# Attention's context: normed by token rows during the last pair of experts, its keys and values multiplied between the norm's transposes

## The reference

```python
x = layer_norm(DEEPNORM_ALPHA * x + g2 * y, ln_ffn_g[layer], ln_ffn_b[layer])   # end of the first block
...
h  = rmsnorm(x, norm_g[i]) * (1 + scale) + shift
hc = rmsnorm(ctx, norm_g[i]) * (1 + cscale) + cshift
a_val, a_gate, q, k, v, b_gate = jnp.split(h @ w_in, EVEN_SPLITS_2, axis=-1)
ck, cv = jnp.split(hc @ w_in[:, EVEN_SPLITS_2[2]:EVEN_SPLITS_2[4]], 2, axis=-1)
```

## Time and profile before

| what | value |
|---|---|
| median of 3 runs (lowest, highest) | 2036.94 us (2034.76, 2041.7) |
| the profiled execution: its own time | 2035.64 us |
| the profiled execution: span | 2033.8 us |
| TensorE busy | 1957.2 us, 96% |
| VectorE busy | 923.7 us, 45% |
| ScalarE busy | 347.5 us, 17% |
| chain that ended last: TensorE, VectorE, issue | 92%, 5%, 1% |

### The profile page before, as it was taken

One profiled execution on the slowest core, in us unless ns is written; L12 is line 12 of the kernel. 1 busy time (PEld: TensorE's weight loads), 2 busy tenths in 40 slices (PEclk: granted clock), 3 DMA queues, 4 the chain that ended last, 5 costly groups with the idle time before them and its releaser, 6 DMA issues.

```text
span 2033.8 us, 23216 instructions
## 1 busy us (share of the span) xinstructions
PE 1957.2 (96%) x8998; PEld 1177.3 (58%) x8998; DVE 923.7 (45%) x1909; ACT 347.5 (17%) x874; POOL 53.9 (3%) x89
## 2 busy tenths in 40 slices
PE   5999999999999989999999999999999989999998
PEld 3886744433433338789967444334333378768875
DVE  6556743422222215768777534222222256653364
ACT  1111311011111103331013110111111131321121
POOL 0100000000000000000000000000000000020000
PEclk9999899999999998999998999999999999999999
DMA  9863588899999974753354888999999866223411
GB/s 405 328 258 133 188 329 361 346 391 423 424 424 420 423 320 151 266 200 132 125 191 187 331 358 346 393 423 423 423 422 423 347 257 235 96 83 132 146 39 42
DMA packets 82107, 576.90 MB, mean 284 GB/s; under 512 B 9148, under 2 KB 11452, under 8 KB 12800
## 3 DMA queue, kind: packets, MB, share of 16 engines
q1 hardware_dynamic: 70992, 494.84, 60.1%
q0 software_dynamic: 10992, 80.43, 10.8%
HBM read 574.17 MB, written 1.06 MB: 283 GB/s over the span
## 4 chain that ended last, share of the span: by engine, by line
PE 92%; DVE 5%; issue 1%; DMA 1%; ACT 1%; DVEq 0%; SPq 0%
PE ps L301 90%; PE ps L305 2%; DVE hma L514 1%; DVE slab L313 1%; DVE slab L1258 0%; DMA slab<-in_ada 0%; DVE hma L313 0%; DVE gds L655 0%; DVE slab L2800 0%; DVE slab L2797 0%; DVE slab L2590 0%; ACT slab L308 0%; DMA wbuf<-in_od_out 0%; DVE wbuf L480 0%; DVE wP L2054 0%
## 5 line engine op out<-in xcount | busy, mean ns | idle before, releaser
L301 PE MATMUL ps<-slab 128*128 128x256 f32 (+7 forms) x1960 | 580.0, 465 | 3.3 <-DVE slab L2074 2.1
L301 PE MATMUL ps<-wbuf,slab 128*64 128x512 f32 (+2 forms) x1584 | 433.9, 591 | 0.1
L301 PEld LDWEIGHTS ps<-slab 128*128 128x128 f32 (+2 forms) x1960 | 289.4, 178 | 219.6 <-issue 199.1
L301 PE MATMUL ps<-hma,wbuf 128*128 128x256 f32 (+1 forms) x1648 | 372.3, 387 | 0.9 <-DVE hma L313 0.9
L301 PEld LDWEIGHTS ps<-hma,wbuf 128*128 128x128 f32 (+1 forms) x1648 | 316.1, 193 | 50.4 <-issue 5.7
L301 PEld LDWEIGHTS ps<-wbuf,slab 128*64 128x64 f32 (+1 forms) x1584 | 147.2, 144 | 238.7 <-issue 237.6
L308 ACT ACTIVATE slab<-ps 128x256 f32<-128x256 f32 (+3 forms) x141 | 64.4, 466 | 1124.1 <-PE ps L301 1124.1
L301 PE MATMUL ps<-wbuf,cst 128*64 128x512 f32 x704 | 190.8, 592 | 0.0
L1536 DVE TENSOR_TENSOR slab<-ps,rs_t 128x512 f32<-128x512 f32 x128 | 88.5, 692 | 216.9 <-PE ps L301 216.9
L1524 DVE TENSOR_TENSOR slab<-ps,slab 128x256 f32<-128x256 f32 x64 | 27.2, 425 | 324.7 <-ACT slab L308 324.4
L301 PE MATMUL ps<-slab,cst 128*64 128x512 f32 (+4 forms) x434 | 134.5, 539 | 7.6 <-ACT slab L308 7.1
(11 more groups left out here) (276 smaller groups left out, 1503.3 us busy)
## 6 DMA issues: line engine op xcount, KB each, us to landing
wbuf<-in_moe_gu SPq DMA_DIRECT2D x170, 1024.0 KB, 9.4
wbuf<-in_moe_d SPq DMA_DIRECT2D x88, 1024.0 KB, 11.0
slab<-in_moe_gu SPq DMA_DIRECT2D x64, 1024.0 KB, 9.9
wbuf<-in_ada POOLq DMA_DIRECT2D x60, 1024.0 KB, 5.2
wbuf<-in_od_in SPq DMA_DIRECT2D x30, 1024.0 KB, 5.0
wbuf<-in_ev_in SPq DMA_DIRECT2D x22, 1024.0 KB, 8.1
wP<-in_moe_gu SPq DMA_DIRECT2D x22, 1024.0 KB, 10.0
slab<-in_moe_d SPq DMA_DIRECT2D x20, 1024.0 KB, 11.2
```

The costliest lines, as they stand in the source:

```text
L301: return e.matmul(o, lhsT, rhs, start=start, stop=stop, skip_group_check=skip)
```

## The change

- SyncE loads the context twice: by token (`a_ct`, new input "ctx") and turned (`a_hc`), behind the experts' last loads. Its wait ahead of the attention's loads is gone, and keys and values are loaded first.
- ScalarE squares the context by token with a running sum and makes the root of each token's mean (`c_rs`), behind its last SiLU. TensorE spreads the two columns of roots over a bank with two products with the identity, ahead of the last pair's down products.
- VectorE norms the context in four parts (`context_dve`): two ahead of the last two scalings, two behind them.
- Keys of the context are multiplied ahead of the transposes of token half 0, values of the context ahead of those of half 1. ScalarE squares and keeps the keys between its two roots (`key_act`).
- In the attention the context's sum of squares and `rms_dve` are gone. Keys and values of x follow each other; VectorE copies the context's values ahead of `rms_dve` for x, and x's values between the third and fourth modulation step, ahead of the first sine.

```diff
-        def res_pe(e, kind, last, rows=None):
+        def res_pe(e, kind, last, rows=None, between=None):
             for m in range(2):
+                if between is not None:
+                    between(m)
                 for f in range(2):
...
             if rows is not None:
                 rows_act(e, rows, g_rows, freed_by)
+            if kind == "m1":
+                key_act(e, 0)
             stats_act(e, kind, 1, eps5)
...
+            if l == 1:
+                e.wait_ge(*on("m_xl", 1, NP - 1))
+                e.dma_start(flat(a_ct), A["ctx"]).then_inc(*Q.arrive("ct", "ctx_t"))
+                e.dma_start(flat(a_hc), A["ctxT"]).then_inc(*Q.arrive("cx", "ctx"))
             over(e, l, over_sp, Q)
...
+                if l == 1 and q == NP - 1:
+                    p = fill_bank(e, ("n_rs", "ac"), ("n_h", "ac", 7))
+                    e.wait_ge(*on("c_rs"))
+                    for m in range(2):
+                        t = mm(e, p[:, m * 128:m * 128 + 128], c_rs[:, m:m + 1].broadcast_to([128, 128]), ident, True, True)
+                    t.then_inc(*P.up("n_rs", "ac"))
...
+            if l == 1:
+                e.preload_act_table_set(LN_EXP)
+                e.wait_ge(*on("landed", "ctx_t"))
+                for m in range(2):
+                    t = afn(e, a_ct[:, m, :], a_ct[:, m, :], ACT.Square, acc=c_ss[:, m:m + 1])
+                t.then_inc(*C.up("c_ss"))
+                e.wait_ge(*C.now)
+                afn(e, c_rs, c_ss, ACT.Ln, scale=1.0 / D, bias=eps6).then_inc(*C.up("c_ln"))
+                e.wait_ge(*C.now)
+                afn(e, c_rs, c_rs, ACT.Exp, scale=-0.5).then_inc(*C.up("c_rs"))
             over(e, l, over_act, C)
...
+        def context_dve(e, parts):
+            if 0 in parts:
+                e.tensor_tensor(comb[:, 3, :], vec[:, 8, :], modc[:, 1, :], ALU.mult).then_inc(*V.up("n_g", "ac"))
+                e.wait_ge(*on("landed", "ctx"))
+                e.wait_ge(*on("n_rs", "ac"))
+            rs = bank("n_rs", "ac")[:, 0:256]
+            for i in parts:
+                o = a_hc[:, 2 * i:2 * i + 2, :]
+                e.tensor_tensor(o, o, bc(rs, 2), ALU.mult).then_inc(*V.up("n_n", "ac", i))
+                e.wait_ge(*V.now)
+                for j in (2 * i, 2 * i + 1):
+                    ts(e, a_hc[:, j, :], a_hc[:, j, :], comb[:, 3, j:j + 1], modc[:, 0, j:j + 1], ALU.mult,
+                       ALU.add).then_inc(*V.up("n_h", "ac", j))
...
                 for f in range(2):
+                    if l == 1 and q == NP - 1:
+                        context_dve(e, (f,))
...
+            if l == 1:
+                context_dve(e, (2, 3))
             over(e, l, over_dve, V)
...
-        A_ORDER = (("a_av", 0), ("a_k",), ("a_q", 0), ("a_q", 1), ("a_q", 2), ("a_v",), ("a_av", 1), ("a_bg", 0),
+        A_ORDER = (("a_k",), ("a_v",), ("a_av", 0), ("a_q", 0), ("a_q", 1), ("a_q", 2), ("a_av", 1), ("a_bg", 0),
...
         def attn_sp(e):
-            e.wait_ge(*on("m_y", 1, NP - 1))
-            e.wait_ge(*on("m_ttc", 1, NP - 1))
-            e.wait_ge(*on("m_ysc", 1, NP - 1, 1))
-            e.dma_start(flat(a_cT), A["ctxT"]).then_inc(*Q.arrive("cx", "ctx"))
...
             rstd_pe(e, "ax", S(7, 8, 256))
-            rstd_pe(e, "ac", S(6, 8, 256))
...
-            both(("a_k",), 1)
-            both(("a_k",), 0)
-            P.also("used", ("a_k",))
+            for key in (("a_k",), ("a_v",)):
+                both(e, key, 1)
+                P.also("used", key)
             plain(("a_q", 0))
...
-            both(("a_v",), 0)
             heads_pe(e, "a_q", 6, S(7, 8, 256))
-            both(("a_v",), 1)
-            P.also("used", ("a_v",))
             plain(("a_av", 1))
...
         def attn_dve(e):
+            value(0)
             rms_dve(e, "ax", xT, 12, 8, hT, lambda i: ("n_x", "m1", 1, i // 2))
-            rms_dve(e, "ac", a_cT, 12, 8, a_hc, lambda i: ("landed", "ctx"), modc, a_cT)
...
-            some(steps, 4)
+            some(steps, 3)
+            value(1)
+            some(steps, 1)
             sin_dve(e, 0)
...
-            value(0)
             some(steps, 3)
             for i in range(3):
                 normed("a_q", a_q, i, S(6, 8, 256))
-            value(1)
...
-            res_pe(e, "m1", True)
+            res_pe(e, "m1", True, None, lambda m: both(e, (("a_k",), ("a_v",))[m], 0))
```

More of the change, by code:

```diff
@@ L1146, in build @@
         NG, NP = NE // 4, NE // 2
+        a_ct, a_hc = S(1, 2, 1024), S(2, 8, 256)
+        c_ss, c_rs = flat(gds[:, 2:4, :])[:, 24:26], flat(gds[:, 2:4, :])[:, 26:28]
         def rows_at(k0, n):
@@ L2119, in rms_dve @@
                         *V.up("n_h", kind, j))
-        a_cT, a_hc = S(5, 8, 256), S(4, 8, 256)
         a_q, a_k, a_v = S(0, 8, 256), S(1, 8, 256), S(2, 4, 256)
@@ L2153, in attn_pool, with both @@
                 ada_load(e, A_ADA[3], q, 2, True)
+        def both(e, key, o):
+            u, src = unit(key, 8, 256), (a_hc, hT)[o]
+            p = fill_bank(e, key + (o,), (key[0] + "c", o))
+            e.wait_ge(*on("landed", key))
+            for m in range(2):
+                for k in range(8):
+                    if o == 0 and m == 0:
+                        e.wait_ge(*on("n_h", "ac", k))
+                    a1, a2 = (u[:, k, m * 128:m * 128 + 128], src[:, k, :]) if key[0] == "a_k" else \
+                        (src[:, k, m * 128:m * 128 + 128], u[:, k, :])
+                    t = mm(e, p[:, m * 256:m * 256 + 256], a1, a2, k == 0, k == 7)
+            t.then_inc(*P.up(*key, o))
         def attn_pe(e):
             rstd_pe(e, "ax", S(7, 8, 256))
-            rstd_pe(e, "ac", S(6, 8, 256))
[L2159 to L2171, removed]
             def plain(key, ready=None):
@@ L2277, in attn_pe, with kept, squared, key_act @@
             banks.ids, banks.i = list(range(8)), 0
+        def kept(e, key, dst, scale=1.0):
+            e.wait_ge(*on(*key))
+            afn(e, flat(dst), bank(*key)[:, :], ACT.Copy, scale=scale).then_inc(*C.up(key[0] + "c", key[1]))
+        def squared(e, key, sq):
+            e.wait_ge(*on(*key))
+            afn(e, flat(sq), bank(*key)[:, :], ACT.Square).then_inc(*C.up("h_sq", *key))
+        def key_act(e, o):
+            squared(e, ("a_k", o), S(5, 8, 256)[:, 2 * o:2 * o + 2, :])
+            kept(e, ("a_k", o), a_k[:, 2 * o:2 * o + 2, :], cv1("kn"))
         def attn_act(e):
             rstd_act(e, "ax", xT, S(7, 8, 256), eps6, lambda i: ("n_x", "m1", 1, i // 2), rs_t[:, 0, 0:256], None)
[L2281 to L2289, removed]
-            def query(i):
[L2292 to L2302, removed]
+            def query(i):
+                squared(e, ("a_q", i), S(7, 8, 256)[:, 2 * i:2 * i + 2, :])
+                kept(e, ("a_q", i), a_q[:, 2 * i:2 * i + 2, :], cv1("qn"))
+            kept(e, ("a_av", 0), a_av)
+            key_act(e, 1)
+            sin_act(e, 0)
             query(0)
@@ L2309, in attn_act @@
             roots_act(e, "a_q", 6, S(6, 8, 256), 1.0 / 128)
-            kept(("a_av", 1), a_ag)
+            kept(e, ("a_av", 1), a_ag)
             def scores(hp):
@@ L2325, in weigh @@
                         *C.up("a_mx", hp, i))
-            kept(("a_bg", 0), a_bg[:, 0:2, :])
+            kept(e, ("a_bg", 0), a_bg[:, 0:2, :])
             scores(0)
-            kept(("a_bg", 1), a_bg[:, 2:4, :])
+            kept(e, ("a_bg", 1), a_bg[:, 2:4, :])
             scores(1)
@@ L2332, in attn_act @@
             weigh(0)
-            kept(("a_bg", 2), a_bg[:, 4:6, :])
+            kept(e, ("a_bg", 2), a_bg[:, 4:6, :])
             e.wait_ge(*C.now)
@@ L2348, in attn_dve, with value @@
         def attn_dve(e):
+            def value(o):
+                e.wait_ge(*on("a_v", o))
+                e.tensor_copy(flat(a_v[:, 2 * o:2 * o + 2, :]), bank("a_v", o)[:, :]).then_inc(*V.up("a_vc", o))
+            value(0)
             rms_dve(e, "ax", xT, 12, 8, hT, lambda i: ("n_x", "m1", 1, i // 2))
-            rms_dve(e, "ac", a_cT, 12, 8, a_hc, lambda i: ("landed", "ctx"), modc, a_cT)
             steps = ada_steps(e, A_ADA[0:3])
@@ L2364, in roped @@
                 e.tensor_tensor(x[:, j, :], x[:, j, :], p[:, 256:512], ALU.add).then_inc(*V.up(done, j))
-            def value(o):
-                e.wait_ge(*on("a_v", o))
-                e.tensor_copy(flat(a_v[:, 2 * o:2 * o + 2, :]), bank("a_v", o)[:, :]).then_inc(*V.up("a_vc", o))
-            some(steps, 4)
+            some(steps, 3)
+            value(1)
+            some(steps, 1)
             sin_dve(e, 0)
@@ L2980, in packed @@
     out["ctxT"] = v["ctx_2"][0].T.reshape(128, 2048)
+    out["ctx"] = v["ctx_2"][0].reshape(2, 128, 1024).transpose(1, 0, 2).reshape(128, 2048)
     out["ada"] = np.concatenate([sections(v["ada_w"]), sections(v["w_mod_2"])])
```

## The result

| | before | after |
|---|---|---|
| median (lowest, highest) | 2037.28 us (2034.76, 2041.7) | 2051.34 us (2049.09, 2053.14) |
| runs | 4 | 4 |
| the profiled execution: its own time, span | 2035.64, 2033.8 us | 2049.09, 2047.3 us |

The ratio is 1.0067, with a 95% interval of 1.0055 to 1.0079: 14 us slower. The forecast was 1.5 us slower, and the time lies above its range.

A forecast was written before the change was run, and what follows sets the result against it. TensorE was taken as the bound, but for the norm between last pair and attention. A gain of 4.8 us against 6.3 lost behind gave +1.5 on the profiled 2035.64: 2037.1, as a median 2038.4; range 2032 to 2046.

The forecast's parts named there:

- What bounds the kernel; what is moved: TensorE is the bound after 1640; the change moves its work into the norm, where it idles.
- The last pair: Last pair of experts: context work makes down products 1.8 us later and the last scaling 2.5 us late.
- The branch: Norm: TensorE's own run-time branch for overflowing experts, hidden before, becomes bare; 3.0 us, bounds 0 and 6.09.
- I price it as VectorE's, 3.0: TensorE's bare branch in the norm is charged like VectorE's 2.97 us, the nearest row.
- rival 2: Norm: loads lengthen TensorE's branch by 3.1, keys run at clock 0.50 (3.4 more), deciding from about 5 us; 2045; chance 0.17.
- Keys 1627.5 to 1634.6: Norm: the product of context and key weights follows TensorE's branch at full clock within these times.
- over the 4.1 us after which the clock fell: Norm before: clock fell 4.1 us after the last scatter product; only a longer idle time would slow the keys.
- The stalls behind: Attention behind the pooling projection: TensorE waits 1.0 ahead of key rotation, 1.3 ahead of query rotations, 3.4 ahead of pooling.
- which takes 5.9 to land: Attention: load of the last part of task 16, issued after the fourth modulation step, lands 5.9 us later.
- The sum: Gain of 4.8 us to the pooling projection's end, less 6.3 lost behind it: 1.5 us slower.
- Rival 1: Attention: VectorE follows after all, so the 4.8 us arrive, at most 8; 2033.6, down to 2030; chance 0.24.
- Rival 3: Last pair: second context load lands at 1620, last scaling 3 us later again; +4.5, 2041.4; chance 0.07.

The follow-up runs named there:

- the fillers: Kernel after plus throwaway TensorE products ahead of the third key rotation, first query rotation and pooling, filling its waits for VectorE; ratio 1.0036 to the kernel before.

## Why the prediction was wrong

- **What bounds the kernel; what is moved.** Right. TensorE is the bound, 14.1 us of its work went from where it was bound into the gap of the norm.
- **The last pair.** Right in kind, a little too dear: down products 1.3 us later (1.8 said), last scaling 1.5 (2.5). The table load and the squares came as worked out (1.28, next operation 0.02 behind it, 1.06 a square).
- **The branch.** The step "I price it as VectorE's, 3.0" failed by 1.0: 4.03 on TensorE. I had named the reason as rival 2 (weights loading during the branch) and still took the quiet row. Holding the loads shows it: 1.71. What else makes it 2.68 in one kernel and 4.93 in another with full queues in both stays open.
- **"Keys 1627.5 to 1634.6", at full clock.** This failed, by 2.7 us: 9.74. Removing the branch gives 7.07. The clock fell while TensorE waited for its branch, and "over the 4.1 us after which the clock fell" was one sample taken for a bound. In the kernel after it had fallen 2.5 us after the last scatter product, and 2.9, 3.4 and 5.0 us after it in three other kernels with the bare branch. So even the 3.0 us that I forecast gave no ground for full clock; no run has a pause of that length there. The sign that I had set for rival 2, a granted clock of 0.50 during the keys, was seen. Rival 2 put 3.1 + 3.4 on this place; 1.0 + 2.7 is what it cost. The pooling projection's end was 12.2 late, not 9.3: -1.0 for the scaling, +1.0 for the branch, +2.7 for the keys, 0.2 unnamed.
- **The stalls behind.** The waits came where they were forecast: VectorE stands still 15.55 us ahead of the values copy (about 15 said), TensorE waits 1.26 ahead of the query rotations (1.3) and 3.17 ahead of the pooling (3.4). The first was 2.75 and not 1.0: "which takes 5.9 to land" was a row of a quieter moment, it took 8.00 here. That the two later stalls hang on the same block was not forecast, and it is not so: with the values copied later they stay (1.60, 3.17).
- **The step that failed most** is the one that is not in the text: what a stall does to the clock. I charged three waits (5.7 us by the list, 6.3 in the sum) and nothing for the half clock behind them. Queries 2 lost 1.7, pooling and gate projection 3.2. With the fillers these 4.9 us vanish while the waits remain.
- **The sum.** Forecast +1.5 within the seam, measured +11.0. Of the 9.5 between, half clock is 7.6 (2.7 + 1.7 + 3.2), the branch 1.0, the load 1.75, the scaling -1.0, the rest 0.2. The other 3 us of the median lie outside the seam, where the forecast put nothing, and stay open. Half clock in the old norm had been credited (5.33 to 3.69), in the new places it was not debited.
- **Rival 1** (VectorE follows) is wrong for this order and right as an idea: with the order changed alone the seam is 0.9 us shorter than before, the time the same. Its price had a slip: 2033.6 takes the 4.8 us from the forecast, which holds 6.3 us of stalls; from the time before it is 2032.1. **Rival 3** (a late context) did not occur in the kernel after: VectorE's first part waited for the spreading products and began 0.11 us behind them, not for the load, and the last scaling was early. In small it came in five of the experiments, where the squares waited 0.5 to 0.9 us for the load. Rival 2's condition of 5 us was not met, but its two halves were each in part.

## What to carry to other kernels

Work moved off a bound engine gives back only what the engines behind can follow; write down the new order of the slowest follower (here VectorE, with its two buffers) before the gain is counted. Charge each new stall of TensorE twice, as its length and as the half clock that may stand behind it: here the stalls of 2.75 and 3.17 us behind the projection brought 4.9 more. Where an engine branches and nothing hides it, keep bulk loads off the queues until it has passed: a hold that ends too early moves them under the branch again (2.68 and 2.89 for 1.71).

## What the runs showed of the hardware

- One taken branch took TensorE 1.71 us with the loads held (81 GB/s in it) and 1.78 with 50 GB/s; with 382 to 420 GB/s it took 2.68, 2.89, 4.03, 4.04, 4.13 and 4.93. So transfers lengthen it, but their rate does not set its length. VectorE took 2.78 with the loads held and 4.95 without. Rows of before had 2.97 and 6.09, with 130 and 355 GB/s moving.
- The clock fell to 0.50 behind a pause of 2.75 us, and behind one of 3.17 that followed one of 1.26; both amid light work (short rotations, the pooling of 64 rows). With these pauses filled it stayed at 1.00. With the loads held a pause of 1.71 did not lower it, but in the 2.20 ahead of the sum of squares it fell; in the kernel after the same pause (2.21) left it at 1.00 (3.69 for the sum).
- A low stretch need not move with the work: it stood from 1626.2 to 1636.5 with the branch and without, so that 2.5 us of earlier start gave only 1.25.
